# Prompt sparse attention with keys on the partitions and two rounded score passes; the causal convolution and silu moved behind the first projection; stores waited for at the end

## What is computed

```python
y = xp[:, 0:T] * w[0]                      # causal_conv, then silu
for j in range(1, CONV_W):
    y = y + xp[:, j:j + T] * w[j]

# compressed branch: means of 32 keys; window branch: last 512 keys; selected branch:
_, idx = lax.top_k(score, min(SEL_TOPK, ns))   # 16 of ns = 16 blocks for the prompt: all of them
s = jnp.einsum('bqghd,bkgd->bghqk', qg, k) * B_SCALE
p = masked_softmax(s, mask)                # per branch
o = jnp.einsum('bghqk,bkgd->bqghd', p, v)
o = gates[..., 0:1] * o_cmp + gates[..., 1:2] * o_sel + gates[..., 2:3] * o_win
```

## Time and profile before

| what | value |
|---|---|
| median of 3 runs | 4640.76 us |
| the profiled execution (its span; no other time is listed for it) | 4641.7 us |
| PE busy | 3957.7 us, 85% |
| DVE, ACT, POOL busy | 1255.5, 843.1, 1228.9 us |
| first projection, 28.7 to 346.7 | 318.0 us |
| even rows, 347.7 to 380.7 | 33.0 us |
| gates, 380.7 to 407.7 | 27.0 us |
| sparse attention of the prompt, 407.7 to 1010.6 | 602.9 us |
| silu, 1010.6 to 1028.2 | 17.6 us |

### The profile page before, as it was taken

How to read it: one execution, slowest core, us unless ns; L and a number is a source line. 1 busy time by engine, 2 the same in 40 slices (tenths; PEclk the granted TensorE clock), 3 DMA queues, 4 the chain that set the end, 5 groups by cost and what they waited for, 6 DMA issues and landing times. The chain is left out here.

```text
span 4641.7 us, 60752 instructions
## 1 busy us (share of the span) xinstructions
PE 3957.7 (85%) x22661; PEld 3606.5 (78%) x22661; DVE 1255.5 (27%) x2404; ACT 843.1 (18%) x1751; POOL 1228.9 (26%) x507
## 2 busy tenths in 40 slices
PE   8994888868878787879999799798677879999897
PEld 8993666646666666869999799798566769999896
DVE  1125664433333321120000321212542320001322
ACT  0002333342222211020000100200552130000002
POOL 3434970000000002323333333243000313333441
PEclk9995866788878775699999899899565889999899
DMA  2112000003323123411111111011001111111111
GB/s 78 45 33 102 1 0 0 0 16 91 91 59 103 54 72 104 130 36 37 45 45 45 34 44 40 25 47 28 1 0 55 59 28 45 46 50 31 44 44 49
DMA packets 313875, 215.85 MB, mean 47 GB/s; under 512 B 27736, under 2 KB 308705, under 8 KB 313468
## 3 DMA queue, kind: packets, MB, share of 16 engines
q1 hardware_dynamic: 298132, 203.69, 15.1%
q10 hardware_dynamic: 13104, 5.87, 0.5%
q0 software_dynamic: 2560, 5.25, 0.4%
HBM read 196.51 MB, written 22.53 MB: 47 GB/s over the span
## 5 line engine op out<-in xcount | busy, mean ns | idle before, releaser
L573 PE MATMUL ps<-X_rounded,up_w_hi 128*128 128x344 f32 x2112 | 678.2, 321 | 31.8 <-DVEq L588 31.8
L575 PE MATMUL ps<-X_rounded,up_w_rounded 128*128 128x344 f32 x2112 | 682.5, 323 | 0.0
L574 PE MATMUL ps<-Xl_ffn,up_w_hi 128*128 128x344 f32 x2112 | 678.3, 321 | 0.0
L573 PEld LDWEIGHTS ps<-X_rounded,up_w_hi 128*128 128x128 f32 x2112 | 398.8, 189 | 32.9 <-DVEq L588 32.9
L575 PEld LDWEIGHTS ps<-X_rounded,up_w_rounded 128*128 128x128 f32 x2112 | 399.8, 189 | 0.0
L574 PEld LDWEIGHTS ps<-Xl_ffn,up_w_hi 128*128 128x128 f32 x2112 | 398.4, 189 | 0.0
L252 PE MATMUL ps<-down_m_hi,down_w_hi 128*128 128x344 f32 x1056 | 343.0, 325 | 59.9 <-POOL down_w_rounded L319 46.8
L1982 POOL DMA_DIRECT2D ns_vp<-in_cache_nsa_kv x80 | 43.8, 547 | 1196.2 <-issue 1174.4
L317 POOL TENSOR_TENSOR up_w_hi<-up_w,ones 128x2048 fp32r<-128x2048 f32 x40 | 183.8, 4595 | 663.2 <-DMA up_w<-in_w_ffn_up 663.2
L254 PE MATMUL ps<-down_m_hi,down_w_rounded 128*128 128x344 f32 x1056 | 341.9, 324 | 0.0
L253 PE MATMUL ps<-F_rounded,down_w_hi 128*128 128x344 f32 x1056 | 340.7, 323 | 0.0
(11 more groups left out here) (487 smaller groups left out, 7894.2 us busy)
## 6 DMA issues: line engine op xcount, KB each, us to landing
X<-in_cache_nsa_kv SPq DMA_DIRECT2D x128, 192.0 KB, 2.4
up_w<-in_w_ffn_gate SPq DMA_DIRECT2D x44, 512.0 KB, 4.1
up_w<-in_w_ffn_up SPq DMA_DIRECT2D x44, 512.0 KB, 5.3
down_w<-in_w_ffn_down SPq DMA_DIRECT2D x32, 704.0 KB, 4.6
in_even_w<-in_w_in_even SPq DMA_DIRECT2D x52, 256.0 KB, 3.0
H<-in_cache_nsa_kv SPq DMA_DIRECT2D x64, 192.0 KB, 2.5
dp_kp_last<-in_cache_nsa_kv SPq DMA_DIRECT2D x64, 192.0 KB, 2.4
in_odd_w<-in_w_in_odd SPq DMA_DIRECT2D x48, 256.0 KB, 3.2
```

The costliest lines, as they stand in the source:

```text
L573: pe.matmul(dst, hi[:, u, part * KD + k, :], xh, start=(k == 0), stop=False)
L574: pe.matmul(dst, hi[:, u, part * KD + k, :], xl, start=False, stop=False)
L575: mm = pe.matmul(dst, lo[:, u, part * KD + k, :], xh, start=False, stop=(k == KD - 1))
```

## The change

1. `load_phase` also loads the 24 old convolution rows and turns them (12 transposes); the convolution weights come with the constants, on ACT's queue.
2. In the first projection DVE applies the convolution to a channel block as soon as it is copied out (12 blocks), and ACT applies silu to 16 blocks. The convolution on POOL and `silu_phase` are gone.
3. `even_rows_phase` stores X first, then the rows; it waits only for two small convolution tails. The copies from DRAM to DRAM are issued last and waited for in `store_phase`. POOL builds VA: the values with a column of ones.
4. `nsa_prompt_phase` is new. Keys lie on the partitions of the scores, and four heads of 128 queries on the free axis. 148 steps (t, g, branch, key block), 6, 10, 14, 18, 22, 24, 26 and 28 of them for the 8 tiles. A step is two rounded (fp32r) matmuls of 512 columns (a third with the mask in 40 steps), one exponential on ACT, and 4 float32 matmuls of 65 columns that give the values and, by the column of ones, the sum. The maxima are found ahead, for the next tile, in 16 halves per tile (head by head, on rounded queries and keys) with DVE's tensor_tensor_reduce, then turned on PE, copied on ACT, and multiplied into rows of the second score operand by POOL ("shift"). No weights are transposed any more. DVE normalises 48 times (t, g, branch).

```diff
@@ load_phase
+            sp.dma_start(conv_rows, r.state_delta_conv[0].rearrange("b j c -> (b j) c")).then_inc(conv_in, 16)
...
@@ project_split_phase(..., convolve=0, lit=0)
+        def _(act):
+            for m in range(convolve):
+                act.wait_ge(conv_ready, m + 1)
+                act.activation(out[:, m, :], acc[:, m % 2, :], ACT.Silu).then_inc(conv_lit, 1)
...
+                v.tensor_copy(r.tail[:, m, :], x[:, T - 3:N])
+                v.tensor_scalar(y, x, w[:, 36 + m:37 + m], None, ALU.mult).then_inc(conv_step, 1)
+                for n, j in enumerate((2, 1, 0)):
...
+                    v.scalar_tensor_tensor(out=y[:, back:T], in0=x[:, 0:T - back],
+                                           scalar=w[:, 12 * j + m:12 * j + m + 1], in1=y[:, back:T], op0=ALU.mult,
+                                           op1=ALU.add)
@@ even_rows_phase
-            sp.dma_start(r.o_win_s[0].rearrange("b w c g d -> b w (c g d)")[:, 0:511, :],
-                         r.state_nsa_win[0].rearrange("b w c g d -> b w (c g d)")[:, 1:512, :]).then_inc(stored, 16)
+            sp.dma_start(r.x_spilled, r.X[:]).then_inc(r.x_out, 16)
...
+            sp.dma_start(r.o_win_s[0].rearrange("b w c g d -> b w (c g d)")[:, 0:511, :],
+                         r.state_nsa_win[0].rearrange("b w c g d -> b w (c g d)")[:, 1:512, :]).then_inc(r.copies_out, 16)
+            r.n_rows_out, r.n_copies_out = late, 2
             sp.wait_ge(stored, 16 * n)
@@ store_phase
+            sp.wait_ge(r.copies_out, 16 * r.n_copies_out)
@@ nsa_prompt_phase, PE
+            def maxima(t, half):
...
+                if index >= 2:
+                    pe.wait_ge(mx_done, index - 1)
...
+            def scores(n):
...
+                if n >= 2:
+                    pe.wait_ge(exped, n - 1)
+                if n == FIRST_OF[t]:
...
+                    pe.wait_ge(shifted, 2 * t + 2)
...
+                pe.matmul(dst, first, QM1[:, t % 2, g], start=True, stop=False)
+                mm = pe.matmul(dst, second, QM2[:, t % 2, g], start=False, stop=mask is None)
+                if mask is not None:
+                    mm = pe.matmul(dst, ident_r[:], heads4(mask[:]), start=False, stop=True)
...
+            def values(n):
+                t, g, br, b, q, first, last = STEPS[n]
+                pe.wait_ge(exped, n + 1)
...
+                for h in H4:
+                    mm = pe.matmul(r.ps[:, 6 + q % 2, 65 * h:65 * h + 65], PT[0:keys, n % 3, h * P:(h + 1) * P], rhs,
+                                   start=(first and h == 0), stop=(last and h == 3), skip_group_check=True)
...
+            for n in range(COUNT):
+                values(n)
+                if n + 2 < COUNT:
+                    scores(n + 2)
...
+                for half in halves_after(n):
+                    maxima(STEPS[n][0] + 1, half)
...
@@ nsa_prompt_phase, DVE
+            def maxima(t, half):
...
+                    v.tensor_tensor_reduce(s_win[:, 0:w], s_win[:, 0:w],
+                                           edge[:] if t >= 4 else diag[:, 1152 - w:1152], -1.0, 3e38, ALU.add,
+                                           ALU.min, neg[:, t % 2, to + 4:to + 5]).then_inc(mx_done, 1)
...
+            def normalise(n):
...
+                kept(v.reciprocal(rec[:], o[:, :, 64]))
...
+                    v.tensor_tensor(part, o[:, :, 0:64], scaled, ALU.mult).then_inc(o_used, 1)
+                    v.wait_ge(o_used, q + 1)
+                    add = v.tensor_tensor(total, total, part, ALU.add)
...
-            silu_phase(nc, r)
```

More of the change, by code:

```diff
@@ new lines, in shift @@
+            def shift(t):
+                pool.wait_ge(neg_kept, t + 1)
+                for g in range(2):
+                    rows = slice(other(g).start, other(g).start + 12)
+                    pool.tensor_tensor(QM2[rows, t % 2, g], heads4(negT[rows, :]),
+                                       own_head[rows, :].unsqueeze(2).to_broadcast([12, 4, P]),
+                                       ALU.mult).then_inc(shifted, 1)
+                    pool.wait_ge(shifted, 2 * t + g + 1)
+            keys(0)
@@ L874, in _ @@
+            shift(0)
+            keys(1)
+            for t in range(1, TT):
+                shift(t)
         @block.tensor
@@ new lines, in _, with queries, keys @@
+            act.preload_act_table_set("natural_log_exp_and_others")
+            act.wait_ge(r.x_out, 16)
+            def queries(t, i):
+                g, rows = i // 2, other(i // 2) if i % 2 else home(i // 2)
+                if t >= 2 and i == 0:
+                    act.wait_ge(st_ready, FIRST_OF[t - 1])
+                act.copy(QM1[rows, t % 2, g], r.H[home(g), Q_B:Q_B + 4, t * P:(t + 1) * P]).then_inc(q_hi, 1)
+            def keys(part):
+                cols = slice(512 * part, 512 * part + 512)
+                for br in range(2):
+                    for g in range(2):
+                        act.copy(KW1[home(g), br, g, cols], r.H[home(g), KEYS[br], cols]).then_inc(k_hi, 1)
@@ L1034, in silu_phase, with queries @@
[L1034 to L1042 removed]
+            def queries(t):
+                v.wait_ge(q_hi, 4 * t + 4)
+                if t >= 2:
+                    v.wait_ge(st_ready, FIRST_OF[t - 1])
+                for g in range(2):
+                    v.tensor_tensor(QM2[home(g), t % 2, g], r.H[home(g), Q_B:Q_B + 4, t * P:(t + 1) * P],
+                                    QM1[home(g), t % 2, g].bitcast(F32), ALU.subtract).then_inc(q_lo, 1)
@@ new lines, in _ @@
+            v.wait_ge(tables_in, 16 * n_tables)
+            v.wait_ge(edges_set, 1)
+            v.wait_ge(neg_zero, 1)
+            queries(0)
+            for half in range(16):
+                maxima(0, half)
+                if half == 7:
+                    keys(0)
+            keys(1)
+            for n in range(COUNT):
+                t, g, br, b, q, first, last = STEPS[n]
+                if last:
+                    normalise(n)
+                for half in halves_after(n):
+                    if half == 0:
+                        queries(t + 1)
+                    maxima(t + 1, half)
```

595 lines of the change are left out of this document (366 added, 229 removed).

## The result

The changed kernel takes 4562.02 us in the median (4554.27 to 4563.1, 4 runs), the kernel before 4640.65; the ratio is 0.983 (0.9816 to 0.9844). It is faster by 78.6 us where 269 were forecast, and lies above the range of 4318 to 4530. The profiled execution is 4559.7 us.

A forecast was written before the change was run, and what follows sets the result against it. The sparse attention, 602.9 us, was held bound by a chain no engine fills. From 4641.7: load +1.5, projection 0, even rows and gates +4, attention −257.5, silu −16.5, sum 4373; forecast 4372, range 4318 to 4530.

The forecast's parts named there:

- The clock of tiles 4 to 7: Sparse attention: 100 steps at full clock, 161 us for these tiles; the rise in mid tile 3 takes 13 off.
- rival 1: Sparse attention: the clock stays at half throughout the stage, 498 us, total 4526; chance 0.28.
- Rival 2: Sparse attention: full clock from tile 1 on, 299 us, total 4327; chance 0.14.
- The price of a step at half clock: Sparse attention: two wide matmuls at 0.42 us and eight float32 records at 0.213 each; 122 us for 48 steps.
- POOL's convolution off the chain: Old sparse attention: POOL's convolution, busy 141 of the first quarter's 150 us, was held not to lengthen the stage.
- Even rows and gates: Barrier 11.5 us earlier, but the gates' loads wait behind the copy: +4 us, bounds −11.5 to +10.
- Rival 4: Gates: the two loads pass the large copy, 15.5 us under the forecast, 4357; no chance of its own.
- The projection: First projection: DVE's convolution work, 6.6 of PE's 11.37 us a chunk, stays hidden: 0 us, bounds 0 to +12.
- rival 5: First projection: DVE becomes the bound, passes of 2.4 us, 15 us a chunk, total 4416; chance 0.04.
- Load, silu, last stores: Load stage +1.5 us, the silu stage gone −16.5, stores waited for at the end 0.
- Rival 3: Sparse attention: DVE bounds the tiles, tensor_tensor_reduce taking 2.28 us per 1,024 columns: +36, total 4409; chance 0.08.
- Rival 6: Sparse attention: DVE's work stands in line with PE's at half clock, slower than before, total 4686; chance 0.03.

The follow-up runs named there:

- k128: The changed kernel with 128 instead of 64 partitions in the maxima's matmuls and the keys' rests built earlier: 4391.52 us, ratio 0.9474.
- wide_values: The changed kernel with each step's values as one wide float32 matmul, the attention output left wrong: 4388.08 us, one run.
- old_attention: The changed kernel with the attention function of before, without its convolution on POOL and without VA: 4596.55 us, ratio 0.9912.
- copies_later: The changed kernel with the two DRAM-to-DRAM copies issued behind the gates' two loads: median 4530.02 us, from 4449.44 to 4546.36.
- narrow: The changed kernel with maxima over only the first 32 keys, still on 64 partitions: 4495.05 us, one run.

## Why the prediction was wrong, step by step

- **The clock of tiles 4 to 7, which I let rise in tile 3: the step that failed.** It went as rival 1, which had 0.28. I had weighed the right row, 1802 to 1924, and argued that the wide passes would outweigh it. `k128` (532 to 356 us with 128 partitions for 64 in the maxima, columns and count the same) and `wide_values` (to 356 with nothing but the form of the values changed) show that it hangs on the stream, not on pauses; by which property of the stream stays open. My 161 us for tiles 4 to 7 were 318 (82.6 + 89.1 + 95.2 + 51.4). In `k128` tiles 4 to 7 take 43.4, 44.8, 48.9 and 41.4, 178.5. A tile from 4 to 6 at half clock thus cost 39 to 46 us more, where I had 20 to 35. Rival 2 falls too: tiles 1 and 2 had 0.53 and 0.61.
- **The price of a step at half clock.** Rival 1 gave 498, the stage took 532. The values were right at 1.73; the 0.13 to 0.17 us that stand open where the kind of matmul changes were left out. In tile 6 that is 95.2 measured, against 26 × 2.55 + 6 × 0.42 + 11.1 + 3.4 = 83.3 by my prices. Tiles 0 to 3 took 180.2 (442.9 to 623.1), where I had 154 − 13. The start took 27.8 instead of 21.5; in it PE's first score pass waited 3.35 us for the first shift alone, where I had 2 with turn and copy, and my 8 for the maxima is 9.6 by its own terms (3.6 for 24 maxima, 2.4 for their columns, 3.6 for their reads).
- **POOL's convolution off the chain: wrong.** I compared quarters of the stage by time, which are not equal work: 498 records of PE in the first, 603 in the third. `old_attention` shows up to 38.6 us. The 2.08 us row was in my hands and I used it for the projection alone. No term of the sum hung on it, since the new attention was priced by itself. The Trainium skill (SBUF — State Buffer, SBUF: two separate sides) has the loser of the shared port block for a whole instruction. The lengthened DVE groups on SBUF, and the unchanged ones on PSUM, agree with it.
- **So what the change earns, by parts**, from the runs (on two chips, each beside its own runs of before): convolution and silu moved, with the stores, 4638.3 to 4596.6, −41.8; the new attention on top of that, 564.3 to 532.1, −32.2, and 4596.6 to 4562.0, −34.5 (−36.8 with each against its own before). The gain forecast for the attention, 257.5, would have been 246.7 (602.9 − 356.2) with the clock of `k128`: the size was that of full clock.
- **Even rows and gates**: right in kind. Forecast +4, from a first gate pass at 387; it began at 390.98, +7.85, and the stages together are 5.7 longer. The Trainium skill (DMA: Bandwidth & Descriptors, Queues, rings and completion order) has each DMA engine consume descriptors in ring order. `copies_later` agrees, 18.97 us against 0.25. Rival 4 falls.
- **The projection**: 0 was right within 1.3 us, and rival 5 falls (the chunks kept to 11.4 us), but the cover is thinner than I said. An undisturbed pass of 1,023 columns takes 1.28 us on 128 partitions; beside POOL's splits a pass of 1,021 took 3.50 and one of 8 columns 2.35. Timeline of DVE in a chunk of the kernel after, and its groups in the projection:

```profile
125.27 1.29 DVE L448 SCALAR_TENSOR_TENSOR in_even_conv<-H,conv_wt,in_even_conv 128x1022 f32<-128x1022 f32 x1
126.47 2.35 DVE L451 SCALAR_TENSOR_TENSOR in_even_conv<-bufT,conv_wt,in_even_conv 128x8 f32<-128x8 f32 x1
128.86 3.50 DVE L448 SCALAR_TENSOR_TENSOR in_even_conv<-H,conv_wt,in_even_conv 128x1021 f32<-128x1021 f32 x1
```
```profile
L448 DVE SCALAR_TENSOR_TENSOR in_even_conv<-H,conv_wt,in_even_conv 128x1023 f32<-128x1023 f32 (+2 forms) x36 | 70.6, 1960 | 1.3
L451 DVE SCALAR_TENSOR_TENSOR in_even_conv<-bufT,conv_wt,in_even_conv 128x8 f32<-128x8 f32 x36 | 33.6, 933 | 0.0
```

  That makes 3 × 1.96 + 3 × 0.93 + 1.52 + 0.17 + 0.75 = 11.1 us a chunk of 11.37, not 6.6.
- **Load, silu, last stores**: near enough. The load cost 0.45 for +1.5 (the projection's first matmul at 29.16, before at 28.71); silu's 17.6 us are gone and the stage behind it is 1.5 longer (649.8, before 648.3), which makes −16.1 for −16.5; the copies were not waited for at the end (from the first store of y to the end 16.9 us, 19.2 before).
- **Rival 3** falls: tensor_tensor_reduce takes 1.23 us for 1,024 columns and 0.14 for its read, the plain rate that the sum had. **Rival 6** falls: the mean step was 3.4 us (498.5 / 148), under 3.9, and PE was busy, not waiting.

## What to carry to other kernels

A stage that becomes bound by TensorE has two prices a factor of two apart, and a busy PE does not settle which: look in the trace for a stretch of the same mix, and give both prices a chance until one is found. If a stream of short matmuls sits at half clock, make its columns wide or put the idle rows of the array to use (128 partitions instead of 64 cost no column here and gave about 170 us) before taking work away. Before an operation is called hidden, compare the same unit of work with and without it; and a small load that starts a chain goes into the queue ahead of a large copy, not behind it.

## What the runs showed of the hardware that was not expected

- PE almost without a pause is not enough for the full clock: 0.50 for over 80 us at a time with PE busy 97 to 98% (tiles 4 to 6 of the changed kernel), 1.00 in the same tiles with the values in wide form.
- Taking columns of matmul away can leave the clock low (`narrow`, 0.60 over the stage, 0.50 in tile 6), and using 128 partitions for 64 at the same columns raise it (`k128`, 0.84).
- A 512-column rounded matmul takes 0.57 us from start to start at half clock when it comes behind float32 matmuls or ahead of 64-partition ones, and 0.43 between rounded ones on 128 partitions.
- An 8-column scalar_tensor_tensor of DVE on SBUF takes 0.21 us alone and 2.35 beside a POOL operation that reads and writes SBUF; DVE's reductions from PSUM beside POOL keep their time.
